# Mixer A's attention steps in an encoder block on eight Trainium2 cores: score of step k+1 issued before PV of step k

## The chip, the cores and the metric

The kernel runs on the eight cores of one Trainium2 chip, four on each of two dies. Every core runs the same program on its own 1024 tokens (a quarter of one of the two sequences) and needs nothing from the others while it runs. The metric is device time in microseconds (us) of the slowest core.

## The reference, cut to what matters

One layer of a bidirectional encoder: an adaLN-modulated RMSNorm, one wide input projection, two attention mixers, gates, an output projection, then a mixture of 64 experts. The change touches mixer A, dilated sliding-window attention with three head groups:

```python
A_PATTERNS = ((128, 1), (512, 4), (2048, 16))     # (window, dilation), 4 heads of 128 each

def dilated_attention(q, k, v, window, dilation):
    # tokens of one residue class modulo dilation form a sequence of their own
    o, lse = banded_attention(split(q), split(k), split(v), (window // 2) // dilation)
...
    # banded_attention: each query sees the keys at most 64 positions away
    sc = jnp.einsum('bhnqd,bhnkd->bhnqk', qb, kwin) * (hd ** -0.5)
    sc = jnp.where(valid, sc, NEG)
    lse = jax.nn.logsumexp(sc, axis=-1)
    p = jnp.exp(sc - lse[..., None])
    o = jnp.einsum('bhnqk,bhnkd->bhnqd', p, vwin)
...
w = jax.nn.softmax(jnp.stack(lses, axis=0), axis=0)           # the groups' weights
o = jnp.sum(w[..., None] * jnp.stack(outs, axis=0), axis=0)
```

The kernel keeps, for each group, the unnormalised sum of exp(score) x V and the sum of exp(score), adds both over the groups, and divides once at the end.

## The kernel before, in words

All data lies in one SBUF arena and eight PSUM banks. The program is written out in Python as five queues, one per engine; `P.op(engine, fn, reads, writes)` appends an instruction to the queue of its engine and works out from the buffers it reads and writes which counts of other engines it has to wait for. An engine runs its queue in the order in which the source appends to it; no scheduler moves anything. A wait stands in front of the instruction that needs it and holds up all that is behind it in that queue.

The stages, in order: conditioning vectors; normalised own tokens; mixer A; keys, values and attention of mixer B; gates and output projection; expert stage with the final norm.

Mixer A works in eight units: four of dilation 16 (four residue classes each), two of dilation 4 (two classes each), two of dilation 1. At the first unit of a dilation the queries are projected for all 1024 tokens. Then each unit projects keys and values, tile by tile of 128 keys (`run_pipeline`, matmuls on L447, transposes on L473), and only when they are all done comes the part that the change rewrites, L689 to L754: a loop over classes, heads h and key tiles m, one step for each. A step is

- S: a score matmul into bank `bi`, keys as rows, queries of one or two 64- or 128-wide blocks as columns (L704, TensorE);
- an exponential from PSUM into a bf16 buffer (L709, ScalarE);
- a multiplication by the band mask and the key-valid column (L718, VectorE);
- PV: for each block one matmul with V into bank 2 or 3 (L730) and one with a matrix of ones into bank 4 or 5 for the sum (L732), TensorE.

After the last key tile of a head the two PSUM results are evicted by ScalarE (L742, L744) into two scratch buffers, and VectorE copies (dilation 16: L747, L749) or adds them (L752, L754) to the accumulators `accO` and `accZ`. The steps per unit are 32 (16 class-heads of 2 key tiles), 24 (8 of 3) and 20 (4 of 5): 128 + 48 + 40 = 216 in all. Score banks 0 and 1, and the two exponential and two mask buffers, are chosen by `bi = (m + h) % 2`.

After the last unit VectorE forms the reciprocal of all of `accZ` (L762) and mixer B begins. Mixer B's own attention (score L871, exponential L874, PV L884 and L886) already issues the score matmul of a step before the PV of the step before it.

The weights of the projections come through a ring of three slots, loaded by GpSimd's queue (L118); a load waits for the matmuls that last read its slot.

Of the kernel before, what the change touches and what calls it, by code (L numbers as in the profile page):

```python
# [7 lines left out]
AF = mybir.ActivationFunctionType  # L8
ALU = mybir.AluOpType
# [11 lines left out]
SCALE = float(HD) ** -0.5  # L21
# [113 lines left out]
def build_nc(stop_after=None, dbg=None):  # L135
    nc = bass.Bass("TRN2", target_bir_lowering=False)
    P = Prog()
# [39 lines left out]
    def V(off, shape, dt=BF16):  # L177
        n = 1
        for s_ in shape[1:]:
            n *= s_  # L180
        assert off % 4 == 0
        assert off + n * (4 if dt == F32 else 2) <= ARENA * 2, (off, shape)
        if dt == F32:
            a = arena[:, off // 2: off // 2 + 2 * n].bitcast(F32)
        else:
            a = arena[:, off // 2: off // 2 + n]
        if len(shape) == 3:
            a = a.rearrange("p (a b) -> p a b", b=shape[2])
        elif len(shape) == 4:
            a = a.rearrange("p (a b c) -> p a b c", b=shape[2], c=shape[3])  # L190
        if shape[0] < 128:
            a = a[0:shape[0]]
        return a

    def emit(dump=None):
        if dump is not None:
            ap, tiles = dump
            ncol = ap.shape[1]
            P.dma("sp", "do", out_d[0:ap.shape[0], 0:ncol], ap, reads=tiles)
        for sn in list(P.cnt.keys()):  # L200
            P.final_wait("sp", sn)
        sem_names = ["pe", "act", "dve"] + ["sp_d%d" % i for i in range(24)] + ["pool_d%d" % i for i in range(24)]
        sems = {n_: es.enter_context(nc.semaphore("s_" + n_)) for n_ in sem_names}
        with nc.Block() as block:
            @block.tensor
            def _(e):
                P.replay("pe", e, sems)

            @block.scalar
            def _(e):  # L210
                P.replay("act", e, sems)

# [46 lines left out]
    t_const = T("const"); t_modT = T("modT"); t_A1 = T("A1"); t_A2 = T("A2"); t_cact = T("cact")  # L259
# [193 lines left out]
    tmp_t = [T("tmp%d" % i) for i in range(4)]  # L453
# [119 lines left out]
    PTA = VA + 8192  # L573
    EXA = PTA + 2048
# [16 lines left out]
    for (gi, items) in units:  # L591
# [6 lines left out]
        def ktsz(m, gi=gi):  # L598
            return 64 if (gi == 2 and m == 1) else 128
# [84 lines left out]
        if stop_after == 'kv':  # L684
            dd = V(ACCO, [128, 2048], F32); t_dd = T('dd')
            P.op('dve', lambda e: e.tensor_copy(out=dd[:, 0:1024], in_=kaT[:, 0, 0:1024]), reads=t_ka, writes=[t_dd])
            P.op('dve', lambda e: e.tensor_copy(out=dd[:, 1024:2048], in_=V(VA, [128, 1024])), reads=t_va, writes=[t_dd])
            return emit((dd, [t_dd]))
        for ii, (cl, b_lo, b_hi) in enumerate(items):  # L689
            qcol0 = cl * nq  # L690
            for h in range(4):
                ob = 2 + (h % 2)
                zb = 4 + (h % 2)
                for m in range(b_lo, b_hi + 1):
                    n = ktsz(m)
                    blocks = [bq for bq in (m - 1, m) if b_lo <= bq < b_hi]
                    c_lo = blocks[0] * qb
                    ncols = len(blocks) * qb
                    bi = (m + h) % 2
                    sb = pbank(bi)  # L700
                    kpos = ii * kstride + (m - b_lo) * 128

                    def f(e, n=n, c_lo=c_lo, ncols=ncols, sb=sb, h=h, qcol0=qcol0, kpos=kpos, kaT=kaT):
                        return e.matmul(sb[0:n, 0:ncols], lhsT=kaT[:, h, kpos:kpos + n],  # L704
                                        rhs=qaT[:, h, qcol0 + c_lo:qcol0 + c_lo + ncols], start=True, stop=True)
                    P.op("pe", f, reads=[t_ka[ii]] + t_qaT, writes=[PB[bi]])
                    ex = V(EXA + bi * 1024, [128, 512])[0:n, 0:ncols]
                    pt_ = V(PTA + bi * 1024, [128, 512])[0:n, 0:ncols]
                    P.op("act", lambda e, ex=ex, sb=sb, n=n, ncols=ncols: e.activation(  # L709
                        out=ex, in_=sb[0:n, 0:ncols], func=AF.Exp, scale=SCALE), reads=[PB[bi]], writes=[exa_t[bi]])  # L710
                    if len(blocks) == 2:
                        mk = mask2[0:n, 0:256]
                    elif blocks[0] == m:
                        mk = mask2[0:n, 128:128 + qb]
                    else:
                        mk = mask2[0:n, 0:qb]
                    kvc = cl * nkt + m
                    P.op("dve", lambda e, pt_=pt_, ex=ex, mk=mk, n=n, kvc=kvc, kvalid=kvalid: e.scalar_tensor_tensor(  # L718
                        out=pt_, in0=ex, scalar=kvalid[0:n, kvc:kvc + 1], in1=mk, op0=ALU.mult, op1=ALU.mult),
                        reads=[exa_t[bi], t_const], writes=[pta_t[bi]])  # L720
                    for bq in blocks:
                        col = bq * qb - c_lo
                        first = (m == bq)
                        last = (m == bq + 1)
                        po_ = pbank(ob)[:, (bq - b_lo) * qb:(bq - b_lo + 1) * qb]
                        pz_ = pbank(zb)[:, (bq - b_lo) * qb:(bq - b_lo + 1) * qb]
                        vv = vslot[(ii, m)]

                        def g(e, po_=po_, pz_=pz_, vv=vv, pt_=pt_, col=col, n=n, first=first, last=last, h=h, qb=qb):
                            e.matmul(po_, lhsT=vv[:, h * 128:(h + 1) * 128], rhs=pt_[:, col:col + qb],  # L730
                                     start=first, stop=last, skip_group_check=True)
                            return e.matmul(pz_, lhsT=ones_bf[0:n, :], rhs=pt_[:, col:col + qb], start=first,  # L732
                                            stop=last, skip_group_check=True)
                        P.op("pe", g, reads=[pta_t[bi], t_va[ii], t_const], writes=[PB[ob], PB[zb]])
                nqc = (b_hi - b_lo) * qb
                po_all = pbank(ob)[:, 0:nqc]
                pz_all = pbank(zb)[:, 0:nqc]
                dO = accO[:, h, :].rearrange("p (u c) -> p c u", c=r)[:, cl, b_lo * qb:b_hi * qb]
                dZ = accZ[:, h, :].rearrange("p (u c) -> p c u", c=r)[:, cl, b_lo * qb:b_hi * qb]
                eo = tmpv[0][:, 0:nqc]  # L740
                ez = tmpv[1][:, 0:nqc]
                P.op("act", lambda e, eo=eo, po_all=po_all: e.activation(out=eo, in_=po_all, func=AF.Identity),  # L742
                     reads=[PB[ob]], writes=[tmp_t[0]])
                P.op("act", lambda e, ez=ez, pz_all=pz_all: e.activation(out=ez, in_=pz_all, func=AF.Identity),  # L744
                     reads=[PB[zb]], writes=[tmp_t[1]])
                if gi == 2:
                    P.op("dve", lambda e, dO=dO, eo=eo: e.tensor_copy(out=dO, in_=eo),  # L747
                         reads=[tmp_t[0]], writes=[t_accO])
                    P.op("dve", lambda e, dZ=dZ, ez=ez: e.tensor_copy(out=dZ, in_=ez),  # L749
                         reads=[tmp_t[1]], writes=[t_accZ])  # L750
                else:
                    P.op("dve", lambda e, dO=dO, eo=eo: e.tensor_tensor(out=dO, in0=dO, in1=eo, op=ALU.add),  # L752
                         reads=[tmp_t[0]], writes=[t_accO])
                    P.op("dve", lambda e, dZ=dZ, ez=ez: e.tensor_tensor(out=dZ, in0=dZ, in1=ez, op=ALU.add),  # L754
                         reads=[tmp_t[1]], writes=[t_accZ])
        prev_kv_tiles = t_ka + t_va + pta_t + exa_t
        if stop_after == 'u0':
            return emit((accO[:, 0, :], [t_accO, t_accZ]))
# [529 lines left out]
```

How the kernel before makes its waits and increments, by code:

```python
    def replay(self, name, e, sems):  # L125
        for wl, fn, inc in self.q[name]:
            for k, v in wl:
                e.wait_ge(sems[k], v)
            if fn is None:
                continue
            ins = fn(e)
            ins.then_inc(sems[inc[0]], inc[1])
```

## Time and profile before

| | before |
|---|---|
| median of 6 runs | 9770.62 us (9679.11 to 10703.73) |
| the profiled execution, device time | 9680.7 us |
| its span, first to last instruction, slowest core | 9679.2 us |
| spans of the eight cores | 9651.3 to 9679.2 us |
| TensorE matmul busy | 7929.6 us, 82% |
| VectorE busy | 3593.4 us, 37% |
| ScalarE busy | 2132.8 us, 22% |
| mean granted TensorE clock, all cores | 0.934 to 0.935 |

How to read the rows further down: times are in us from the first instruction, unless ns is written. PE is TensorE's matmuls, PEld its weight loads, DVE VectorE, ACT ScalarE, POOL GpSimd. L730 is line 730 of the kernel before. A granted clock of 1.0 is 2.4 GHz, 0.5 is 1.2 GHz. In a timeline row the start time comes first, then the duration, engine, line, operation, output and input; in brackets how long the engine had been idle, and what ended that.

### The profile page before, as it was taken

The page shows a single profiled execution, that of the slowest core. Times are in us where ns is not written, and L with a number is a line of the kernel's source. Part 1 is how long each engine was busy: PE and PEld are TensorE (multiplying, and loading weights), DVE is VectorE, ACT ScalarE, POOL GpSimd, SP SyncE. Part 2 cuts the span into 40 slices and gives each one's busy share as a digit, 9 for nine tenths or more (in the row PEclk, how much of TensorE's full clock was granted, in tenths as well). Part 3 has the DMA queues.
Part 4 walks back from the last instruction along what each step waited for, and adds up shares of the span by engine and source line. Part 5 has one row for each costly group of instructions (what it writes and reads, how often), then busy time and mean ns, then how long its engine had stood idle before and what let it go on. Part 6 is the DMA issues. An engine that isn't in the chain of part 4 may idle for free.

```text
span 9679.2 us, 104693 instructions; the slowest of 8 cores (9651.3 to 9679.2 us)
## 1 busy us (share of the span) xinstructions
PE 7929.6 (82%) x37040; PEld 3549.6 (37%) x37040; DVE 3593.4 (37%) x4682; ACT 2132.8 (22%) x4075; POOL 289.0 (3%) x284
## 2 busy tenths in 40 slices
PE   0135656476777799759999999999999999999998
PEld 0122323232222234324444444444444444444443
DVE  3443334453111111244333334444444433334444
ACT  0124534465666651020000000000000000000001
POOL 0000000000000001000000000000000000000000
PEclk9997777688888999879999999999999999999999
DMA  7541123121000027534444444444444444444443
GB/s 207 170 136 36 48 63 77 56 68 45 13 4 13 9 21 74 90 54 73 76 79 74 73 73 78 79 79 79 79 79 76 74 78 76 73 73 75 79 79 83
DMA packets 505629, 694.53 MB, mean 72 GB/s; under 512 B 129440, under 2 KB 443296, under 8 KB 492960
## 3 DMA queue, kind: packets, MB, share of 16 engines
q0 software_dynamic: 451584, 476.37, 31.9%
q1 hardware_dynamic: 53536, 211.46, 6.7%
q8 instruction: 309, 5.06, 0.2%
q14 instruction: 200, 1.64, 0.1%
HBM read 1155.75 MB, written 8.39 MB: 120 GB/s over the span
## 4 chain that ended last, share of the span: by engine, by line
PE 72%; ACT 8%; DMA 7%; issue 6%; DVE 6%; ACTq 0%; DVEq 0%; SPq 0%; POOLq 0%; POOL 0%
PE psum L1151 37%; PE psum L1174 19%; PE psum L447 6%; PE psum L884 3%; DMA arena<-w_ada 3%; DMA arena<-w_in 2%; ACT arena L874 2%; PE psum L886 2%; PE psum L871 2%; DVE arena L398 2%; ACT arena L396 1%; PE psum L1026 1%; DVE arena L319 1%; DMA arena<-w_b_up 1%; ACT arena L376 1%
## 5 line engine op out<-in xcount | busy, mean ns | idle before, releaser
L1151 PE MATMUL psum<-arena 128*128 128x512 bf16 x16640 | 3603.2, 379 | 0.0
L1151 PEld LDWEIGHTS psum<-arena 128*128 128x128 bf16 x16640 | 1628.4, 98 | 1963.9 <-issue 1.6
L1174 PE MATMUL psum<-arena 128*128 128x512 bf16 x8320 | 1806.3, 379 | 0.0
L1179 DVE SCALAR_TENSOR_TENSOR arena<-psum,arena 128x512 f32<-128x512 f32 x2048 | 1533.0, 750 | 239.4 <-DVE arena L1179 14.5
L1161 DVE TENSOR_TENSOR arena<-arena,psum 128x512 bf16<-128x512 f32 x520 | 357.3, 687 | 2943.8 <-PE psum L1151 2943.8
L1159 ACT ACTIVATE arena<-psum 128x512 f32<-128x512 f32 x520 | 310.5, 597 | 5041.6 <-PE psum L1151 5041.6
L1174 PEld LDWEIGHTS psum<-arena 128*128 128x128 bf16 x8320 | 814.1, 98 | 981.7
L447 PE MATMUL psum<-arena 128*128 128x512 bf16 (+1 forms) x3648 | 923.6, 416 | 214.9 <-DVE arena L520 96.4
L874 ACT ACTIVATE arena<-psum 128x512 bf16<-128x512 f32 x1024 | 605.4, 597 | 296.0 <-PE psum L871 270.1
L447 PEld LDWEIGHTS psum<-arena 128*128 128x128 bf16 (+1 forms) x3648 | 383.4, 107 | 708.6 <-issue 374.7
L884 PE MATMUL psum<-arena 128*128 128x512 bf16 x1024 | 410.0, 400 | 266.8 <-ACT arena L874 251.4
L393 PE MATMUL psum<-arena 128*128 128x128 bf16 (+1 forms) x1504 | 118.4, 245 | 454.8 <-ACT arena L412 388.1
L886 PE MATMUL psum<-arena 128*128 128x512 bf16 x1024 | 408.7, 399 | 0.0
L871 PE MATMUL psum<-arena 128*128 128x512 bf16 x1024 | 407.1, 398 | 0.0
L884 PEld LDWEIGHTS psum<-arena 128*128 128x128 bf16 x1024 | 99.9, 98 | 684.8 <-issue 677.3
L118 POOL DMA_DIRECT2D arena<-w x192 | 195.0, 1016 | 5160.1 <-PE psum L1151 3494.8
L398 DVE TENSOR_TENSOR arena<-arena 128x2048 bf16<-128x2048 bf16 x94 | 198.3, 2110 | 346.8 <-ACT arena L396 346.8
L890 DVE RECIPROCAL arena<-psum 128x512 f32<-128x512 f32 x32 | 107.4, 3357 | 564.7 <-PE psum L886 564.7
L376 ACT ACTIVATE arena<-arena 128x2048 bf16<-128x2048 f32 x102 | 194.0, 1902 | 519.3 <-DMA arena<-xr 505.3
L319 DVE SCALAR_TENSOR_TENSOR arena<-arena 128x1536 f32<-128x1536 f32 x120 | 218.1, 1818 | 209.9 <-DMA arena<-w_ada 209.2
L730 PE MATMUL psum<-arena 128*128 128x128 bf16 (+2 forms) x256 | 58.7, 245 | 288.0 <-DVE arena L718 288.0
L329 PE MATMUL psum<-arena 128*128 128x1 f32 x192 | 41.2, 352 | 307.2 <-DVE arena L319 307.2
(119 smaller groups left out, 3822.4 us busy)
## 6 DMA issues: line engine op xcount, KB each, us to landing
arena<-w POOLq DMA_DIRECT2D x192, 2048.0 KB, 15.0
arena<-w_ada SPq DMA_DIRECT2D x128, 768.0 KB, 5.1
arena<-xr SPq DMA_DIRECT2D x78, 1024.0 KB, 5.0
arena<-w_in POOLq DMA_DIRECT2D x15, 2048.0 KB, 22.7
arena<-w_in POOLq DMA_DIRECT2D x32, 512.0 KB, 6.7
arena<-xr SPq DMA_DIRECT2D x16, 512.0 KB, 5.0
arena<-tabB SPq DMA_DIRECT2D x64, 128.0 KB, 2.0
arena<-w_b_up POOLq DMA_DIRECT2D x16, 512.0 KB, 6.7
```

The lines of the kernel that those rows point to most:

```text
L319: P.op("dve", lambda e, a=a, st=st, k=k: e.scalar_tensor_tensor(out=a, in0=st, scalar=c_act[:, k:k + 1], in1=a, op0=ALU.mult, op1=ALU.add) ...
L398: P.op("dve", lambda e: e.tensor_tensor(out=htmp[:, :, 0:n], in0=htmp[:, :, 0:n], in1=Asc.unsqueeze(2).to_broadcast([128, 16, n]), op=ALU. ...
L447: ins = e.matmul(po[0:n, :], lhsT=hT_ap[:, k, 0:n], rhs=wv[:, k, :], start=(k == 0), stop=(k == 15))
L871: P.op("pe", lambda e: e.matmul(pbank(sbk), lhsT=kbT[:, kvh, t * 128:(t + 1) * 128], rhs=qbT[:, hh, half * 512:(half + 1) * 512], start=Tr ...
L874: P.op("act", lambda e: e.activation(out=ptb[pi], in_=pbank(sbk), func=AF.Exp, scale=SCALE), reads=[PB[sbk]], writes=[ptb_t[pi]])
L884: e.matmul(pbank(ob), lhsT=vB[:, t, kvh * 128:(kvh + 1) * 128], rhs=ptb[pi], start=(t == 0), stop=(t == 31))
L886: return e.matmul(pbank(zb), lhsT=ones_bf, rhs=ptb[pi], start=(t == 0), stop=(t == 31))
L1151: ins = e.matmul(pbank(bank), lhsT=wsrc[:, k, fc * 128:(fc + 1) * 128], rhs=h2T[:, k, hs], start=(k == 0), stop=(k == 15))
L1159: P.op("act", lambda e, st=st, ba=ba: e.activation(out=st, in_=pbank(ba), func=AF.Silu), reads=[PB[ba]], writes=[stt])
L1161: P.op("dve", lambda e, st=st, bu=bu, fc=fc, hs=hs: e.tensor_tensor(out=hidT[:, fc, hs], in0=st, in1=pbank(bu), op=ALU.mult), reads=[stt, ...
L1174: ins = e.matmul(pbank(bank), lhsT=hidT[:, fc, j * 128:(j + 1) * 128], rhs=w2v[:, fc, cs], start=(fc == 0), stop=(fc == 3))
L1179: P.op("dve", lambda e, bank=bank, j=j, cs=cs, ex_i=ex_i: e.scalar_tensor_tensor(out=x1[:, j, cs], in0=pbank(bank), scalar=gate[:, j, ex_i ...
```

## The change

The nested loop becomes a flat list of steps and two functions. `S_step(k)` appends the score matmul, the exponential and the masking of step k; `PV_step(k)` appends its PV matmuls (now as one operation with one wait and one signal, where a step of two blocks had two) and, at the last key tile of a head, the evictions and accumulations. A last loop calls `S_step(k + 1)` ahead of `PV_step(k)`. The buffers alternate with the step's number. Shapes, operands and the number of instructions stay.

```diff
-        for ii, (cl, b_lo, b_hi) in enumerate(items):
-            qcol0 = cl * nq
-            for h in range(4):
-                for m in range(b_lo, b_hi + 1):
...
-                    bi = (m + h) % 2
...
-                    P.op("pe", f, reads=[t_ka[ii]] + t_qaT, writes=[PB[bi]])
...
-                    for bq in blocks:
...
-                        P.op("pe", g, reads=[pta_t[bi], t_va[ii], t_const], writes=[PB[ob], PB[zb]])
+        steps = []
+        for ii, (cl, b_lo, b_hi) in enumerate(items):
+            for h in range(4):
+                for m in range(b_lo, b_hi + 1):
+                    steps.append((ii, cl, b_lo, b_hi, h, m))
+
+        def S_step(k, steps=steps, kaT=kaT, t_ka=t_ka, kvalid=kvalid, qb=qb, nq=nq, nkt=nkt, kstride=kstride, ktsz=ktsz):
+            ii, cl, b_lo, b_hi, h, m = steps[k]
...
+            bi = k % 2
+            sb = pbank(bi)
...
+                 reads=[t_ka[ii]] + t_qaT, writes=[PB[bi]])
...
+            P.op("act", lambda e: e.activation(out=ex, in_=sb[0:n, 0:ncols], func=AF.Exp, scale=SCALE),
+                 reads=[PB[bi]], writes=[exa_t[bi]])
...
+                 reads=[exa_t[bi], t_const], writes=[pta_t[bi]])
+            return (pt_, blocks, c_lo, n, bi)
+
+        def PV_step(k, info, steps=steps, vslot=vslot, t_va=t_va, qb=qb, r=r, gi=gi):
+            ii, cl, b_lo, b_hi, h, m = steps[k]
+            pt_, blocks, c_lo, n, bi = info
+            ob = 2 + (h % 2)
+            zb = 4 + (h % 2)
...
+            P.op("pe", g, reads=[pta_t[bi], t_va[ii], t_const], writes=[PB[ob], PB[zb]])
+            if m == b_hi:
...
+                P.op("act", lambda e: e.activation(out=eo, in_=po_all, func=AF.Identity),
                     reads=[PB[ob]], writes=[tmp_t[0]])
...
+        infos = {0: S_step(0)}
+        for k in range(len(steps)):
+            if k + 1 < len(steps):
+                infos[k + 1] = S_step(k + 1)
+            PV_step(k, infos[k])
```

What moves, on TensorE, in the first dilation 4 unit (steps A, B, C of a head with score widths 128, 256, 128; L704 becomes L705, L730 and L732 become L739 and L741). Before, one head:

```order
L704 MATMUL psum<-arena 128x128
L730 MATMUL psum<-arena 128x128
L732 MATMUL psum<-arena 128x128
L704 MATMUL psum<-arena 128x256
L730 MATMUL psum<-arena 128x128
L732 MATMUL psum<-arena 128x128
L730 MATMUL psum<-arena 128x128
L732 MATMUL psum<-arena 128x128
L704 MATMUL psum<-arena 128x128
L730 MATMUL psum<-arena 128x128
L732 MATMUL psum<-arena 128x128
```

With the change, at the same place, from the score matmul of B to that of the next head's B:

```order
L705 MATMUL psum<-arena 128x256
L739 MATMUL psum<-arena 128x128
L741 MATMUL psum<-arena 128x128
L705 MATMUL psum<-arena 128x128
L739 MATMUL psum<-arena 128x128
L741 MATMUL psum<-arena 128x128
L739 MATMUL psum<-arena 128x128
L741 MATMUL psum<-arena 128x128
L705 MATMUL psum<-arena 128x128
L739 MATMUL psum<-arena 128x128
L741 MATMUL psum<-arena 128x128
L705 MATMUL psum<-arena 128x256
```

Before, the score matmul of a step stands directly in front of its own PV pair or pairs; now the PV of the step before stands between them.

On ScalarE, at the start of the first dilation 16 unit (exponential L709, now L710; evictions L742 and L744, now L753 and L755; a 64x64 exponential belongs to a head's second step). Before:

```order
L709 ACTIVATE arena<-psum 128x64
L709 ACTIVATE arena<-psum 64x64
L742 ACTIVATE arena<-psum 128x64
L744 ACTIVATE arena<-psum 128x64
L709 ACTIVATE arena<-psum 128x64
```

With the change:

```order
L710 ACTIVATE arena<-psum 128x64
L710 ACTIVATE arena<-psum 64x64
L710 ACTIVATE arena<-psum 128x64
L753 ACTIVATE arena<-psum 128x64
L755 ACTIVATE arena<-psum 128x64
L710 ACTIVATE arena<-psum 64x64
```

The first exponential of the next head has moved ahead of the two evictions of this one; the second still stands behind them. VectorE's queue (masking L718, now L719; copies L747 and L749, now L758 and L759) changes in the same way:

```order
L719 SCALAR_TENSOR_TENSOR arena<-arena 128x64
L719 SCALAR_TENSOR_TENSOR arena<-arena 64x64
L719 SCALAR_TENSOR_TENSOR arena<-arena 128x64
L758 COPY arena<-arena 128x64
L759 COPY arena<-arena 128x64
L719 SCALAR_TENSOR_TENSOR arena<-arena 64x64
```

The masking of the next head's first step stands ahead of the copies of this head, that of its second step behind them. The queues of GpSimd and SyncE, which issue the DMAs, do not change.

## Rows read from the trace of the kernel before

**Rows 1.** Windows by stage: span, length, busy per engine (x instructions), PEclk, DMA share, GB/s.
```profile
620.00:1850.00 1230.00, 726.34 (x4099) 372.75 (x4098) 457.73 (x971) 560.89 (x1053) 9.38 (x8) 0.73 0.23 57
```

**Rows 2.** Windows of three score stretches, columns PE, PEld, DVE, ACT, POOL, PEclk, DMA, GB/s.
```profile
772.00:825.00 53.00, 14.44 (x100) 8.19 (x100) 15.27 (x64) 15.59 (x71) 0.00 (x0) 0.53 0.00 1
1394.00:1449.00 55.00, 14.13 (x90) 7.36 (x87) 17.71 (x40) 15.30 (x46) 0.00 (x0) 0.52 0.00 1
1797.00:1844.00 47.00, 13.31 (x83) 7.28 (x83) 13.21 (x28) 12.72 (x30) 0.00 (x0) 0.50 0.18 30
```

**Rows 3.** Waits from 700 to 1900 us: in total, times, longest.
```profile
PE psum L730 <- DVE arena L718: 288.0, 216, 3.7
```

**Rows 4.** Timeline of a dilation 16 unit: start, duration, engine, instruction, idle before.
```profile
788.54 0.21 PE L730 MATMUL psum<-arena 128*128 128x64 bf16 x1 [1.28 <-DVE arena L718]
...
789.84 0.21 PE L730 MATMUL psum<-arena 64*128 64x64 bf16 x1 [0.84 <-DVE arena L718]
...
790.03 0.23 PE L704 MATMUL psum<-arena 128*128 128x64 bf16 x1
...
790.64 0.22 ACT L709 ACTIVATE arena<-psum 128x64 bf16<-128x64 f32 x1
...
791.11 0.28 DVE L718 SCALAR_TENSOR_TENSOR arena<-arena 128x64 bf16<-128x64 bf16 x1
...
791.54 0.21 PE L730 MATMUL psum<-arena 128*128 128x64 bf16 x1 [1.28 <-DVE arena L718]
```

**Rows 5.** Timeline of a dilation 4 unit, first PV matmul of steps C, A, B, C.
```profile
1541.42 0.26 PE L730 MATMUL psum<-arena 128*128 128x128 bf16 x1 [1.22 <-DVE arena L718]
...
1543.90 0.27 PE L730 MATMUL psum<-arena 128*128 128x128 bf16 x1 [2.00 <-DVE arena L718]
...
1545.94 0.27 PE L730 MATMUL psum<-arena 128*128 128x128 bf16 x1 [1.46 <-DVE arena L718]
...
1547.86 0.26 PE L730 MATMUL psum<-arena 128*128 128x128 bf16 x1 [1.22 <-DVE arena L718]
```

**Rows 6.** Timeline of a dilation 1 unit, first PV matmul of steps A to E, A.
```profile
1810.67 0.26 PE L730 MATMUL psum<-arena 128*128 128x128 bf16 x1 [2.39 <-DVE arena L718]
...
1812.73 0.27 PE L730 MATMUL psum<-arena 128*128 128x128 bf16 x1 [1.46 <-DVE arena L718]
...
1814.99 0.26 PE L730 MATMUL psum<-arena 128*128 128x128 bf16 x1 [1.46 <-DVE arena L718]
...
1817.25 0.27 PE L730 MATMUL psum<-arena 128*128 128x128 bf16 x1 [1.46 <-DVE arena L718]
...
1819.16 0.27 PE L730 MATMUL psum<-arena 128*128 128x128 bf16 x1 [1.22 <-DVE arena L718]
...
1822.03 0.27 PE L730 MATMUL psum<-arena 128*128 128x128 bf16 x1 [2.39 <-DVE arena L718]
```

**Rows 7.** Timeline of GpSimd's queue, one row; then windows of the stretch behind it.
```profile
1227.18 1.14 POOL L118 DMA_DIRECT2D arena<-w_in  x1 [2.31 <-PE psum L473]
...
1240.00:1250.00 10.00, 2.64 (x18) 1.50 (x18) 3.44 (x15) 2.90 (x15) 0.00 (x0) 0.50 1.22 197
1250.00:1260.00 10.00, 3.06 (x21) 1.77 (x21) 2.96 (x13) 2.34 (x12) 0.00 (x0) 0.50 0.13 22
```

**Rows 8.** Timeline of VectorE after the last score stretch.
```profile
1844.42 25.75 DVE L762 RECIPROCAL arena<-arena 128x4096 f32<-128x4096 f32 x1
```

**Rows 9.** Groups by line and shape: busy, mean ns of one, idle before.
```profile
L874 ACT ACTIVATE arena<-psum 128x512 bf16<-128x512 f32 x1024 | 605.4, 597 | 296.0 <-PE psum L871 270.1 <-ACT arena L874 1.1 <-PE psum L886 0.7
...
L742 ACT ACTIVATE arena<-psum 128x512 f32<-128x512 f32 x8 | 4.8, 597 | 9.6 <-PE psum L732 9.6
```

**Rows 10.** Window in mixer B's attention, columns as in the other windows.
```profile
2400.00:2500.00 100.00, 72.36 (x277) 24.31 (x276) 17.14 (x22) 62.32 (x127) 0.00 (x0) 0.87 0.02 5
```

**Rows 11.** Timeline of TensorE, score matmuls at the full and the half clock.
```profile
1527.11 0.22 PE L704 MATMUL psum<-arena 128*128 128x128 bf16 x1
...
1541.59 0.31 PE L704 MATMUL psum<-arena 128*128 128x128 bf16 x1
```

More of the change, by code:

```diff
@@ L688, in build_nc @@
             return emit((dd, [t_dd]))
+        steps = []
         for ii, (cl, b_lo, b_hi) in enumerate(items):
-            qcol0 = cl * nq
-            for h in range(4):
-                ob = 2 + (h % 2)
-                zb = 4 + (h % 2)
-                for m in range(b_lo, b_hi + 1):
[L695 to L698, printed above, removed]
-                    bi = (m + h) % 2
[L700 to L705, printed above, removed]
-                    P.op("pe", f, reads=[t_ka[ii]] + t_qaT, writes=[PB[bi]])
[L707 to L720, printed above, removed]
-                    for bq in blocks:
[L722 to L733, printed above, removed]
-                        P.op("pe", g, reads=[pta_t[bi], t_va[ii], t_const], writes=[PB[ob], PB[zb]])
@@ new lines, in build_nc @@
+            for h in range(4):
[3 more added lines that the diff above has]
+            ii, cl, b_lo, b_hi, h, m = steps[k]
+            n = ktsz(m)
+            blocks = [bq for bq in (m - 1, m) if b_lo <= bq < b_hi]
+            c_lo = blocks[0] * qb
+            ncols = len(blocks) * qb
+            bi = k % 2
+            sb = pbank(bi)
+            kpos = ii * kstride + (m - b_lo) * 128
+            qcol0 = cl * nq
+            P.op("pe", lambda e: e.matmul(sb[0:n, 0:ncols], lhsT=kaT[:, h, kpos:kpos + n],
+                                          rhs=qaT[:, h, qcol0 + c_lo:qcol0 + c_lo + ncols], start=True, stop=True),
+                 reads=[t_ka[ii]] + t_qaT, writes=[PB[bi]])
+            ex = V(EXA + bi * 1024, [128, 512])[0:n, 0:ncols]
+            pt_ = V(PTA + bi * 1024, [128, 512])[0:n, 0:ncols]
+            P.op("act", lambda e: e.activation(out=ex, in_=sb[0:n, 0:ncols], func=AF.Exp, scale=SCALE),
+                 reads=[PB[bi]], writes=[exa_t[bi]])
+            if len(blocks) == 2:
+                mk = mask2[0:n, 0:256]
+            elif blocks[0] == m:
+                mk = mask2[0:n, 128:128 + qb]
+            else:
+                mk = mask2[0:n, 0:qb]
+            kvc = cl * nkt + m
+            P.op("dve", lambda e: e.scalar_tensor_tensor(out=pt_, in0=ex, scalar=kvalid[0:n, kvc:kvc + 1], in1=mk,
+                                                         op0=ALU.mult, op1=ALU.mult),
+                 reads=[exa_t[bi], t_const], writes=[pta_t[bi]])
+            return (pt_, blocks, c_lo, n, bi)
@@ new lines, in PV_step, with g @@
+        def PV_step(k, info, steps=steps, vslot=vslot, t_va=t_va, qb=qb, r=r, gi=gi):
[3 more added lines that the diff above has]
+            zb = 4 + (h % 2)
+            vv = vslot[(ii, m)]
+            def g(e):
+                ins = None
+                for bq in blocks:
+                    col = bq * qb - c_lo
+                    first = (m == bq)
+                    last = (m == bq + 1)
+                    po_ = pbank(ob)[:, (bq - b_lo) * qb:(bq - b_lo + 1) * qb]
+                    pz_ = pbank(zb)[:, (bq - b_lo) * qb:(bq - b_lo + 1) * qb]
+                    e.matmul(po_, lhsT=vv[:, h * 128:(h + 1) * 128], rhs=pt_[:, col:col + qb],
+                             start=first, stop=last, skip_group_check=True)
+                    ins = e.matmul(pz_, lhsT=ones_bf[0:n, :], rhs=pt_[:, col:col + qb], start=first,
+                                   stop=last, skip_group_check=True)
+                return ins
+            P.op("pe", g, reads=[pta_t[bi], t_va[ii], t_const], writes=[PB[ob], PB[zb]])
+            if m == b_hi:
@@ L741, in build_nc @@
                 ez = tmpv[1][:, 0:nqc]
-                P.op("act", lambda e, eo=eo, po_all=po_all: e.activation(out=eo, in_=po_all, func=AF.Identity),
+                P.op("act", lambda e: e.activation(out=eo, in_=po_all, func=AF.Identity),
                      reads=[PB[ob]], writes=[tmp_t[0]])
-                P.op("act", lambda e, ez=ez, pz_all=pz_all: e.activation(out=ez, in_=pz_all, func=AF.Identity),
+                P.op("act", lambda e: e.activation(out=ez, in_=pz_all, func=AF.Identity),
                      reads=[PB[zb]], writes=[tmp_t[1]])
                 if gi == 2:
-                    P.op("dve", lambda e, dO=dO, eo=eo: e.tensor_copy(out=dO, in_=eo),
+                    P.op("dve", lambda e: e.tensor_copy(out=dO, in_=eo), reads=[tmp_t[0]], writes=[t_accO])
+                    P.op("dve", lambda e: e.tensor_copy(out=dZ, in_=ez), reads=[tmp_t[1]], writes=[t_accZ])
+                else:
+                    P.op("dve", lambda e: e.tensor_tensor(out=dO, in0=dO, in1=eo, op=ALU.add),
                          reads=[tmp_t[0]], writes=[t_accO])
-                    P.op("dve", lambda e, dZ=dZ, ez=ez: e.tensor_copy(out=dZ, in_=ez),
+                    P.op("dve", lambda e: e.tensor_tensor(out=dZ, in0=dZ, in1=ez, op=ALU.add),
                          reads=[tmp_t[1]], writes=[t_accZ])
[L751 to L755, printed above, removed]
+        infos = {0: S_step(0)}
[3 more added lines that the diff above has]
+            PV_step(k, infos[k])
         prev_kv_tiles = t_ka + t_va + pta_t + exa_t
```

## The prediction, made before the changed kernel was run

> **What bounds the kernel now.** I read the table by stage first, because the change touches one stage only. The front of the layer, 620 to 1850 us, is 1230 us long and TensorE is busy for 726 us of it at a mean granted clock of 0.73 [rows 1]: no engine bounds it, so it must be bound by waits between engines. Then I looked for the eight stretches in it that hold the mixer A score and PV steps, one per unit. Three of them stand in [rows 2], each marked out from the first score matmul to the last accumulate: 53 us for one of the four units of dilation 16 (the others are 51 to 52), 55 us for one of the two of dilation 4 (the other too), 47 us for one of the two of dilation 1 (the other 48). Together that is some 412 us. In each, TensorE, VectorE and ScalarE are each busy for 13 to 18 us out of about 50, and the granted clock is 0.50 to 0.53, the lower of the two levels (1.2 GHz). A third of the time for each of three engines is the picture of a chain in which one works while the others wait. The table of waits names the last link: TensorE waited 216 times, 288 us in all, for the masking on VectorE before a PV matmul [rows 3]. 216 is the number of steps (128 + 48 + 40).
>
> The timeline shows the chain instruction by instruction. In a dilation 16 unit a head has two steps. From the PV of the first to the PV of the second is 1.30 us (788.54 to 789.84); from there to the next head's first PV it is 1.70 us (789.84 to 791.54), because the ScalarE queue holds the two evictions before the next exponential (790.64) and the VectorE queue the two copies before the next masking (791.11) [rows 4]. So a head costs 3.00 us. In a dilation 4 unit the three steps A, B, C of a head give C to next A 2.48, A to B 2.04, B to C 1.92, together 6.44 us [rows 5]. In a dilation 1 unit the five steps A to E give 2.06, 2.26, 2.26, 1.91 and, over the evictions, 2.87, together 11.36 us [rows 6]. Each of these intervals is one full pass: PV, score matmul, exponential, masking, PV.
>
> **The change, part by part.** It adds and removes no arithmetic. Each score matmul, exponential and masking is put one step earlier in the three queues, ahead of the PV of the step before. The interval that I called one pass now leads from PV(k) to PV(k+2): behind PV(k) on TensorE stands S(k+2), then the exponential and the masking of k+2, and PV(k+2) waits for that. Two such chains, of the even and the odd steps, run interleaved. Nothing else becomes a dependence: the score banks and the two pairs of intermediate buffers already alternate, and S(k+2) writes the bank whose reader, the exponential of k, was done before PV(k) could start.
>
> Dilation 16, 64 heads in four units. With two steps a head, the odd chain carries every eviction, so its pass stays 1.70 us; the even chain needs 1.30 us and fits beside it. A head costs 1.70 instead of 3.00 us. Per unit, before: 1.30 + 15 x 3.00 = 46.3 us from first to last PV. After: an estimated 0.4 us from PV 0 to PV 1 (a PV and a score matmul, 0.19 each in [rows 4]; the chains start together, with no eviction there yet), then 15 x 1.70, together 25.9. Saved 20.4 per unit, 81.6 in four.
>
> Dilation 4, 16 heads in two units. With three steps a head, a chain takes every second step: A to C, C to the next head's B, B to the A after that. In two heads that is three passes, one over an eviction, one from each kind of step; I take the three intervals of [rows 5] for them, 6.44 us, though a pass over the eviction now lands on the wider B and one from A on the narrower C, which moves tenths from one link to another. So a head costs 3.22. Before: 2.04 + 1.92 + 7 x 6.44 = 49.0 us; after about 1.7 + 7 x 3.22 = 24.2. Saved 24.8 per unit, 49.6 in two.
>
> Dilation 1, 8 heads in two units. In the same way a chain needs two heads for its five passes, and a head costs 11.36 / 2 = 5.68. Before: 8.5 + 3 x 11.36 = 42.6; after A to C to E, 4.0, + 3 x 5.68 = 21.0. Saved 21.6 per unit, 43.1 in two.
>
> **Sum:** 81.6 + 49.6 + 43.1 = 174 us, so that the 412 us become 238. The table load and first step of each unit and its last eviction stay as they are. One PV operation per step instead of one per query block takes a semaphore increment off TensorE in 40 steps; I cost that at nothing, since the masking before it ends the wait.
>
> What lies behind the score stretches comes earlier by the same amounts, and I looked for what it could run into. Two 2 MB weight loads are issued just before the last dilation 16 stretch begins, the later at 1227, and have landed soon after 1250: the DMA share is 1.22 from 1240 to 1250 and 0.13 after that [rows 7]. Before, that stretch ends at 1280; after the change, 20 us sooner, near 1260, and the loads feed the key and value projections, which come after the query projections. The same pair exists before the last dilation 4 stretch. After the last stretch VectorE has its 25.75 us reciprocal [rows 8] with TensorE idle; it moves forward whole and covers what the last weight load still needs. The long expert stage is untouched. So all of it arrives at the end.
>
> The unknown cost is what a link takes when the other chain works beside it; no row of these stretches shows it. From below it is the link as measured. From above I take the links that already have other work in the queue: 1.70 against 1.30, 2.48 against 1.92, 2.87 against 1.91. The nearest row for an instruction is in mixer B, which does issue one step ahead: its exponential of 128x512 takes 597 ns, as does the 128x512 eviction of mixer A with nothing beside it [rows 9]. I therefore take the links as measured.
>
> The clock is the other unknown. The stretch of [rows 2] has TensorE 14.44 of 53 us busy, 27%, at 0.53; mixer B has 72% busy at 0.87 [rows 10]. After the change it would be 14.4 of about 32, 46%. That is nearer to the 27% row, so I leave the clock where it is. The page "TensorE: Matmul & The Clock Gate" of the Trainium skill, Part 1: The HAM clock gate, says that the slow rate is the default and sustained activity releases it. By that rule the denser stretch could run at 2.4 GHz and the sum would be the first rival's; by the rows it is 174 us.
>
> **The rivals.**
> 1. The clock rises in the denser stretches. The score matmul 128x128 takes 0.22 us at the full clock and 0.31 at half [rows 11], and the step from PV to the score matmul would halve too (0.19 in [rows 4], more with two blocks): about 0.25 us a link. One chain has 108 links, so 27 us more are gained: 9479 us. For it: the share goes from 27 to 46%. Against: it is still far from 72%.
> 2. Each head's evictions hold up both chains, not one. The exponential of k+1 is ahead of the evictions in the queue, but if it comes late, the chains fall into step and lose their interleaving. Priced: 0.65 us per dilation 16 head (a second pass of 1.30, half hidden), 64 x 0.65 = 42; 0.56 per dilation 4 head and 0.96 per dilation 1 head, 9 + 8; together 59, which leaves 115 us of gain: 9565 us. Against it: VectorE, the busiest of the two, has 15.27 us of work in what would be 32.
> 3. The program order changes but the waits stay as serial as now, since they count instructions of an engine and not buffers. Then the time is as before, 9681. Against it: the listing shows S(k+1) and its exponential ahead of everything that depends on PV(k).
> 4. Slower. All three engines now touch the score buffers and PSUM in the same microsecond; if that lengthens their instructions and handovers, the score stretches, 238 us by the links, pass 412 + 20 us only from a factor of 1.8 on. At a factor of 1.9 the time would be 9721. Against it: the two 597 ns of [rows 9].
>
> **How the numbers follow.** The profiled execution took 9680.7 us (span 9679.2); 9680.7 - 174 = 9506 us, against that execution and not against the median of the runs shown, which is 90 us above it; the three lowest of the six runs lie within 4 us. My chances: forecast 0.67, rival 1 0.15, rival 2 0.12, rival 3 0.03, rival 4 0.03. Low end: rival 1 with a little more, 9470. High end: half of the gain lost, 87 us, beyond rival 2 and short of rival 3: 9595. Faster by over 0.2% (19 us, about what a measurement of this kernel can tell from no change) are the first three, 0.94; within it 0.03; slower 0.03.
>
> **What would show it.** The eight score stretches should be about 31, 30 and 26 us long by dilation; TensorE's wait for the masking should fall from 288 to near 115 us. In the timeline of a dilation 16 unit PV to PV should alternate between some 0.4 and 1.3 us, with 1.70 a head; an exponential should start before the PV of the step before it. The stretches between should keep their lengths. The prediction is wrong if a head of dilation 16 takes over 2.3 us, if the clock leaves 0.5, or if the stage behind a score stretch starts with a wait for a load that it did not have.

## The result, and the profile after

| | before | with the change |
|---|---|---|
| median of all runs | 9861.73 us (20 runs) | 9538.78 us (10 runs) |
| lowest run | 9675.03 us | 9501.16 us |
| profiled execution, device time | 9680.7 us | 9506.79 us |
| ratio to the kernel before | | 0.9843, 95% interval 0.98 to 0.9886 |
| eight score stretches, slowest core | 412 us | 239.6 us |

In many runs the cores of one die, or of both, show a lower granted clock and a longer span, with any of the kernels, so the medians hold such runs; below, spans and score stretches are those of a die without them. A score stretch is, as in [rows 2], the time from the first score matmul of a unit to its last accumulate.

The profiled execution fell by 174 us, which was the forecast. On each core the eight score stretches became 172 us shorter; on the slowest core the first of them also began 3 us earlier than before, at 769.6 in place of 772.6 us, and what runs before it is not touched by the change. The windows of one stretch of each dilation, which answer to [rows 2] (columns PE, PEld, DVE, ACT, POOL, PEclk, DMA share, GB/s):

```profile
769.00:801.00 32.00, 12.13 (x100) 7.47 (x100) 14.55 (x64) 14.92 (x71) 0.00 (x0) 0.54 0.01 2
1311.00:1342.00 31.00, 12.77 (x90) 7.81 (x86) 16.69 (x40) 14.83 (x46) 0.00 (x0) 0.56 0.00 1
1643.00:1671.00 28.00, 12.46 (x84) 7.94 (x84) 13.75 (x29) 14.06 (x33) 0.00 (x0) 0.50 0.30 51
```

From first score matmul to last accumulate the eight take 31.3, 31.6, 31.1 and 31.0, then 30.9 and 30.9, then 26.4 and 26.4 us. The instructions per engine are the same as in [rows 2] (in the first, 100, 64 and 71 on TensorE, VectorE and ScalarE); the length is not. The clock is still the lower one. TensorE's wait for the masking, 288 us in [rows 3], is now (in total, times, longest):

```profile
PE psum L739 <- DVE arena L719: 124.4, 121, 3.6
```

It was forecast near 115 us. It has fallen from 216 times to 121: most PVs of the other chain no longer wait. The timeline of a dilation 16 unit shows it (start, duration, engine, instruction; idle time before it in brackets), one head and the start of the next, to be held against [rows 4]:

```profile
785.72 0.21 PE L739 MATMUL psum<-arena 64*128 64x64 bf16 x1 [0.97 <-DVE arena L719]
...
785.91 0.26 PE L705 MATMUL psum<-arena 128*64 128x64 bf16 x1
...
786.11 0.23 PE L739 MATMUL psum<-arena 128*128 128x64 bf16 x1
...
786.19 0.22 ACT L753 ACTIVATE arena<-psum 128x64 f32<-128x64 f32 x1 [0.94 <-PE psum L705]
...
786.53 0.42 ACT L710 ACTIVATE arena<-psum 64x64 bf16<-64x64 f32 x2
...
787.00 0.53 DVE L719 SCALAR_TENSOR_TENSOR arena<-arena 64x64 bf16<-64x64 bf16 x2
...
787.42 0.21 PE L739 MATMUL psum<-arena 64*128 64x64 bf16 x1 [0.97 <-DVE arena L719]
```

From the PV that ends a head (785.72) to the next one that does (787.42) are 1.70 us, the length of the pass over the evictions in [rows 4]; the first-step PV follows 0.39 us behind (786.11) without a wait. Two exponentials and two maskings now run as pairs ("x2") behind the evictions. The same for dilation 4 and dilation 1 (the first PV matmul of a head's second step, one head apart; the row at 1322.92 is the first head's step C, used further down):

```profile
1322.44 0.26 PE L739 MATMUL psum<-arena 128*128 128x128 bf16 x1 [0.94 <-DVE arena L719]
...
1322.92 0.31 PE L739 MATMUL psum<-arena 128*128 128x128 bf16 x1
...
1325.77 0.26 PE L739 MATMUL psum<-arena 128*128 128x128 bf16 x1 [0.94 <-DVE arena L719]
...
1653.29 0.27 PE L739 MATMUL psum<-arena 128*128 128x128 bf16 x1 [1.41 <-DVE arena L719]
...
1659.15 0.27 PE L739 MATMUL psum<-arena 128*128 128x128 bf16 x1 [1.11 <-DVE arena L719]
```

A head costs 3.33 us (forecast 3.22, before 6.44 by [rows 5]) and 5.86 (forecast 5.68, before 11.36 by [rows 6]).

Nothing is given back. From the first score to the last accumulate the slowest core took 1071.7 us before and 900.5 with the change. On average over the eight cores what lies between the eight stretches takes 660 us before and after, what lies between the last accumulate and the expert stage 2407 and 2408 us, and the expert stage 5361 us in both. A window of it with the change, all matmuls:

```profile
4026.00:9326.00 5300.00, 5252.03 (x24397) 2384.85 (x24397) 2167.55 (x2663) 325.74 (x531) 191.90 (x189) 0.99 0.46 76
```

### The profile page after: what moved, and what is told of

Read it like the earlier page. It is cut to its first block, busy times and chain, and to the rows that moved or that the text cites. A ratio compares the mean times of both kernels' runs of the same rounds, so it can differ in the third digit from the quotient of the medians.

```text
span 9505.2 us, 105002 instructions; the slowest of 8 cores (9470.2 to 9505.2 us)
## 1 busy us (share of the span) xinstructions
PE 7908.0 (83%) x37040; PEld 3547.2 (37%) x37040; DVE 3589.4 (38%) x4682; ACT 2127.4 (22%) x4075; POOL 289.0 (3%) x284
## 4 chain that ended last, share of the span: by engine, by line
PE 73%; ACT 8%; DMA 8%; issue 5%; DVE 5%; ACTq 0%; DVEq 0%; SPq 0%; POOLq 0%; POOL 0%
PE psum L1165 38%; PE psum L1188 19%; PE psum L447 6%; DMA arena<-w_ada 3%; PE psum L898 3%; ACT arena L888 2%; DMA arena<-w_in 2%; PE psum L900 2%; DVE arena L398 2%; PE psum L885 2%; ACT arena L396 1%; PE psum L1040 1%; DVE arena L319 1%; DMA arena<-w_b_up 1%; ACT arena L376 1%
## 5 line engine op out<-in xcount | busy, mean ns | idle before, releaser
L1153 DVE TENSOR_TENSOR arena<-arena 128x8192 bf16<-128x8192 bf16 x65 | 287.0, 4415 | 0.0
```

## The experiments

The theory: a score stretch is a chain of passes, and the gain is that a pass now leads two steps on. Its rivals: the gain came with the other edits; an engine binds; the clock rose. All runs, with the mean length of a score stretch by dilation and the sum of the eight, and the median span of a die's cores (the mean of the two dies where both can be used). The spans carry some noise of their own, since the first score stretch starts anywhere from 750 to 784 us; the sums of the stretches agree within 0.5 us from core to core.

| run | dilation 16, 4, 1 (us) | sum | span |
|---|---|---|---|
| before | 51.7, 55.1, 47.6 | 412 | 9664 |
| with the change | 31.3, 30.9, 26.4 | 239.6 | 9493 |
| e1 order undone, rest kept | 55.6, 55.3, 47.6 | 428.3 | 9677 |
| e2 evictions a step later | 28.6, 31.5, 25.6 | 228.7 | 9483 |
| e3 two steps ahead | 22.3, 26.7, 20.6 | 183.7 | 9429 |
| e5 extra matmuls | 31.4, 30.9, 26.4 | 240.0 | 9494 |
| e9 as e1, late wait last | 49.0, 51.1, 43.7 | 385.5 | 9621 |
| e7 the change, late wait last | 28.2, 29.4, 25.0 | 221.7 | 9467 |
| e8 as e3, late wait last | 19.7, 25.0, 19.5 | 167.7 | 9414 |
| e10 as e8, whole program | 19.7, 24.9, 19.8 | 168.1 | 9385 |
| e12 before, late wait last, whole program | 48.8, 51.4, 43.7 | 385.4 | 9594 |
| e11 is e10 again | the same | 167.9 | 9387 |

**The order alone undone.**

```diff
-        infos = {0: S_step(0)}
         for k in range(len(steps)):
-            if k + 1 < len(steps):
-                infos[k + 1] = S_step(k + 1)
-            PV_step(k, infos[k])
+            PV_step(k, S_step(k))
```

> The changed kernel with the order alone undone: each step's score part is issued directly before its own PV part; the buffers by step number and the single PV operation per step stay. Chain theory (the gain is that a pass PV to score to exponential to masking leads to the step after next): the eight score stretches go back to about 52, 55 and 48 us by dilation, 412 in all, and the time to 9680 us, ratio 1.00 against the kernel before. Rival (part of the gain is in what rode along, fewer waits per step and alternating buffers): the stretches stay well under 412, say 330 to 390, and the time 25 to 90 us under the kernel before.

The stretches went back beyond 412, to 428.3 us: the gain is the order's, and what rode along costs 16 us, all of it in dilation 16, 0.25 us a head. The second step of a head shows where. Before (score matmul, exponential, masking; the PVs at both ends, 788.54 and 789.84, stand in [rows 4]):

```profile
788.74 0.26 PE L704 MATMUL psum<-arena 128*64 128x64 bf16 x1
789.10 0.22 ACT L709 ACTIVATE arena<-psum 64x64 bf16<-64x64 f32 x1 [1.23 <-PE psum L704]
789.41 0.28 DVE L718 SCALAR_TENSOR_TENSOR arena<-arena 64x64 bf16<-64x64 bf16 x1 [1.02 <-ACT arena L709]
```

In this run (PV of the first step, score matmul, exponential, masking, PV):

```profile
787.00 0.21 PE L739 MATMUL psum<-arena 128*128 128x64 bf16 x1 [1.27 <-DVE arena L719]
...
787.20 0.26 PE L705 MATMUL psum<-arena 128*64 128x64 bf16 x1
787.67 0.22 ACT L710 ACTIVATE arena<-psum 64x64 bf16<-64x64 f32 x1 [1.34 <-PE psum L705]
788.13 0.28 DVE L719 SCALAR_TENSOR_TENSOR arena<-arena 64x64 bf16<-64x64 bf16 x1 [1.27 <-ACT arena L710]
788.55 0.21 PE L739 MATMUL psum<-arena 64*128 64x64 bf16 x1 [1.09 <-DVE arena L719]
```

The pass takes 1.55 us (787.00 to 788.55) where [rows 4] have 1.30: score matmul to exponential 0.47 in place of 0.36, exponential to masking 0.46 in place of 0.31. The listing of the queues with their waits, for the exponential and the masking of that step, before and in this run:

```
L709 ACTIVATE arena<-psum 64x64 [waits s_pe]
L718 SCALAR_TENSOR_TENSOR arena<-arena 64x64 [waits s_act]

L710 ACTIVATE arena<-psum 64x64 [waits s_pe,s_act,s_dve]
L719 SCALAR_TENSOR_TENSOR arena<-arena 64x64 [waits s_act,s_dve,s_pe]
```

With `bi = (m + h) % 2` the buffers of the dilation 16 steps ran 0, 1, 1, 0, 0, 1, 1, 0: the second step of a head took the buffer that the first step of the head before had used, and a count waited for earlier covered it. With `k % 2` it takes the buffer of the step two before, which no earlier wait covers: two more waits on each of the two instructions, met long ago, but standing behind the one that comes late. That gave a new theory, tried further down.

**Evictions a step later.** The part of `PV_step` from `if m == b_hi` on becomes `EV_step`:

```diff
             PV_step(k, infos[k])
+            if k >= 1:
+                EV_step(k - 1)
+        for k in range(len(steps) - 1, len(steps)):
+            EV_step(k)
```

> The changed kernel with each head's two evictions and two accumulations issued one step later, behind the exponential and masking of the step after next. Chain theory (evictions lie in the pass of the odd chain): a head costs about 1.35 to 1.45 us in dilation 16 in place of 1.70, 3.0 in place of 3.33 in dilation 4, 5.4 in place of 5.86 in dilation 1; the stretches add up to some 210 us in place of 240 and the time is about 9477. Rival (ScalarE or VectorE throughput already sets the step): no change, 240 and 9507.

Between the two: 11 us gained where 30 were expected, and dilation 4 got 0.6 us a unit longer. In dilation 16 most heads of the first unit now take 1.54 or 1.55 us. One pass of the first steps' chain:

```profile
779.94 0.21 PE L739 MATMUL psum<-arena 128*128 128x64 bf16 x1 [0.62 <-ACT arena L758]
...
780.07 0.21 PE L705 MATMUL psum<-arena 128*128 128x64 bf16 x1
...
780.49 0.22 ACT L710 ACTIVATE arena<-psum 128x64 bf16<-128x64 f32 x1 [0.45 <-DVE arena L763]
...
780.95 0.29 DVE L719 SCALAR_TENSOR_TENSOR arena<-arena 128x64 bf16<-128x64 bf16 x1 [0.40 <-PE psum L705]
...
781.49 0.21 PE L739 MATMUL psum<-arena 128*128 128x64 bf16 x1 [0.63 <-ACT arena L758]
```

So the evictions did lie in the pass of the change, 1.70 us, and without them it is about what a pass without evictions took in the first run, 1.55. The expectation had started from the 1.30 of [rows 4], which lacks the added waits: 0.42 us from score matmul to exponential and 0.46 to the masking are 0.21 more than there. Another 0.11 lie between masking and PV (0.54 in place of 0.43), where the PV's wait ends, by the trace, with the eviction L758 that frees its bank; PV to score matmul is 0.07 less. This kernel was not run with another order of waits. In dilation 4 the move only shifted the load: a head takes 3.35 us in place of 3.33, and the second of its two additions is now directly followed on VectorE, with no idle time, by the masking of a later step.

```profile
1322.72 0.59 DVE L768 TENSOR_TENSOR arena<-arena 128x256 f32<-128x256 f32 x1
1323.23 0.33 DVE L719 SCALAR_TENSOR_TENSOR arena<-arena 128x128 bf16<-128x128 bf16 x1
```

**Two steps ahead.** Three score banks (0, 1, 6), three pairs of intermediate buffers:

```diff
-            bi = k % 2
-            sb = pbank(bi)
+            bi = k % 3
+            sbi = (0, 1, 6, 7)[bi]
+            sb = pbank(sbi)
...
-        infos = {0: S_step(0)}
+        infos = {j: S_step(j) for j in range(2)}
         for k in range(len(steps)):
-            if k + 1 < len(steps):
-                infos[k + 1] = S_step(k + 1)
+            if k + 2 < len(steps):
+                infos[k + 2] = S_step(k + 2)
```

> The changed kernel with the score part issued two steps ahead, three score banks and three pairs of intermediate buffers. Chain theory: the same pass now leads to the third step, so a dilation 16 head costs (1.30 + 1.70) / 3 = 1.00 us in place of 1.70, or 1.1 if VectorE's 0.92 us of work per head begins to bind; dilation 4: 2.2 to 2.4 in place of 3.33 (VectorE has 2.09 us of work per head); dilation 1: 3.8 to 4.1 in place of 5.86. Stretches about 170 us, time about 9437. Rival (an engine or the in-order queues bind after one step of lookahead): under 15 us gained, over 9490.

183.7 us, 56 gained where the pure chain gave 70: after the change the passes still bound, no engine did. In a dilation 16 stretch of 22 us VectorE and ScalarE are now busy for 13 each, but that they filled up is not what kept the 14 us back: with the same work a further run below gains 16 by the order of the waits alone.

**Extra matmuls, for the clock.** Ahead of the second PV of each dilation 16 head:

```diff
+            if gi == 2 and steps[k][5] == steps[k][2]:
+                def warm(e):
+                    for _ in range(2):
+                        ins = e.matmul(pbank(7)[:, 0:512], lhsT=ones_bf, rhs=hT_own[:, 0, 0:512], start=True, stop=True)
+                    return ins
+                P.op("pe", warm, reads=[t_const] + hto_t, writes=[PB[7]])
             PV_step(k, infos[k])
```

> The changed kernel with two extra matmuls of 128x512 into an idle bank ahead of the second PV of each head in dilation 16 only, where TensorE waits 0.97 us a head anyway; they do work that nothing reads. If activity sets the clock, the granted clock of the four dilation 16 stretches rises from 0.54 to over 0.8, and at a price of 0.2 us a pass their length falls from 31.3 to about 28 us each. If the clock stays at 0.54, the extra matmuls take 0.85 us of the 0.97 and the stretches stay at 31 to 33 us. The four stretches of dilation 4 and 1 stay as they are in both cases, 30.9 and 26.4.

The window of the first stretch:

```profile
769.00:800.00 31.00, 24.75 (x127) 10.92 (x126) 14.87 (x64) 14.61 (x70) 0.00 (x0) 0.53 0.01 2
```

TensorE is busy for 24.75 of 31 us in place of 12.13 of 32, and the granted clock is 0.53; the stretch keeps its length, 31.4 us against 31.3. At its start TensorE waits 2.85 us (to 772.41); from there to the last PV it is never idle for more than 0.47 us at a time, and from 771 to 800 us the granted clock is 0.50. What a link would cost at the full clock was therefore not measured.

**Order of waits, serial kernel.** A single edit in how the waits of one instruction are listed, switched on for mixer A's steps:

```diff
-        for t in reads:
-            if t.w is not None:
-                need(*t.w)
+        if not self.reads_last:
+            for t in reads:
+                if t.w is not None:
+                    need(*t.w)
         for t in writes:
...
+        if self.reads_last:
+            for t in reads:
+                if t.w is not None:
+                    need(*t.w)
```

> The serial kernel of the first run (428 us of score stretches: 16 us more than before, all in dilation 16) with one more edit, in mixer A's steps alone: where an instruction waits for several counts, the wait for the operand that it reads, which comes last, is put behind the waits for the buffer that it overwrites, which were met long before. The same waits stay. Wait-order theory (each wait that stands behind the late one costs about 0.07 us, and the change added two of them to the exponential and two to the masking of every second step in dilation 16): exponential to masking falls from 0.46 to about 0.32 us, score matmul to exponential from 0.47 to 0.36, in every step; some 0.25 us per step, 216 steps, so the stretches take about 375 us, dilation 16 about 48 each. Rival (the order of waits is free, and the 16 us come from the banks and buffers themselves): 428 us, no change.

385.5 us in place of 428.3: 43 gained of the 53 expected. The same instructions as above:

```profile
778.28 0.21 PE L746 MATMUL psum<-arena 128*128 128x64 bf16 x1 [1.10 <-DVE arena L726]
...
778.47 0.26 PE L712 MATMUL psum<-arena 128*64 128x64 bf16 x1
778.83 0.22 ACT L717 ACTIVATE arena<-psum 64x64 bf16<-64x64 f32 x1 [1.16 <-PE psum L712]
779.15 0.28 DVE L726 SCALAR_TENSOR_TENSOR arena<-arena 64x64 bf16<-64x64 bf16 x1 [1.02 <-ACT arena L717]
779.57 0.21 PE L746 MATMUL psum<-arena 64*128 64x64 bf16 x1 [0.84 <-DVE arena L726]
```

Score matmul to exponential 0.36 (was 0.47), exponential to masking 0.32 (was 0.46): the pass takes 1.29 us (778.28 to 779.57), as in [rows 4], with the same three waits on each as in the first run. Two waits behind the late one cost 0.11 and 0.14 us here.

**Order of waits, the change.** The same edit.

> The changed kernel with the same edit of the order of waits in mixer A's steps. Wait-order theory: each of the 108 passes on a chain gets some 0.25 us shorter, less where the instruction sits in the queue behind an eviction: a dilation 16 head about 1.40 us in place of 1.70, dilation 4 about 3.0 in place of 3.33, dilation 1 about 5.3 in place of 5.86; stretches about 212 us in place of 240, time about 9479. Rival (order is free): 240 and 9507.

221.7 us: 18 gained of the 28 expected. One dilation 16 head, PV to PV of the second steps, is 1.52 us in place of 1.70. That instructions behind an eviction gain less, as the expectation allowed, fits this, but no run shows it by itself:

```profile
768.26 0.21 PE L746 MATMUL psum<-arena 64*128 64x64 bf16 x1 [0.80 <-DVE arena L726]
...
769.78 0.21 PE L746 MATMUL psum<-arena 64*128 64x64 bf16 x1 [0.80 <-DVE arena L726]
```

**Order of waits, two steps ahead.** The same edit on the kernel of e3.

> The kernel with the score part two steps ahead (184 us of score stretches) with the same edit of the order of waits in mixer A's steps. If the passes still bind with three chains, a third of 0.25 us per step is gained, 216 x 0.08 = 18 us: about 166 us. If an engine's queue binds instead (VectorE has 0.92 us of work per head in dilation 16 and the head takes about 1.36), under 5 us are gained, 180 or more, unless the waits themselves fill the queue, and then the gain is larger, down to about 155.

167.7 us, 16 gained of the 18 expected. A dilation 16 head is down to 0.95 us (PV of first steps):

```profile
776.16 0.21 PE L747 MATMUL psum<-arena 128*128 128x64 bf16 x1
...
777.11 0.21 PE L747 MATMUL psum<-arena 128*128 128x64 bf16 x1
```

**Order of waits in the whole program.** On the kernel of e3, and on the kernel before; the reads simply follow the writes for every instruction.

> The kernel with the score part two steps ahead and the order of waits turned round in the whole program, not in mixer A's steps alone. The score stretches should equal those of the kernel with the edit in mixer A alone. Outside, about 2300 us of the program are bound by handovers (key and value production, mixer B's attention, where TensorE waits 251 us for the exponential in 1024 steps): at 0.07 us per wait behind the late one, 20 to 100 us are gained. If the order is free, nothing: the time is that of two steps ahead, about 9450.

> The kernel before, in its serial order, with the order of waits alone turned round in the whole program. Wait-order theory: the score stretches go from 412 to about 385 us, what the serial kernel with the late wait last had (there the two added waits no longer cost anything, so both kernels meet), and outside them some 25 us are gained, as between the two kernels with two steps ahead: about 9630 us on an undisturbed die against 9680. If the order matters only where steps overlap: 412 and 9680.

The score stretches came out as expected, 168.1 and 385.4 us. The second equals the 385.5 of the serial kernel with the late wait last: in that order of waits the two serial kernels meet, so the 16 us between them (428.3 and 412) were the place of the added waits and nothing else that rode along. Outside the stretches, measured from the first score matmul to the end as a mean over cores, the edit gave 29 us between e8 and e10 (8651 to 8622) and some 40 on the kernel before (8900 to 8833, less 27 in the stretches). Of these, 31 and 37 us lie between the last accumulate of mixer A and the expert stage; the expert stage gained nothing.

**The best version, once more.**

> The kernel with the score part two steps ahead and the late wait last in the whole program, once more, for a ratio against the kernel before. From its first look: 168 us of score stretches, about 9400 us on undisturbed dies, ratio 0.971 against the kernel before; the changed kernel stands at 0.982.

The medians of the two dies' spans were 9385.9 and 9388.0 us. The lowest of six runs took 9400.52 us; the three lowest runs of the kernel before beside it took 9668.49, 9669.19 and 9670.83: 0.972. That rests on one run of the best version, and no interval was given for it.

## What the prediction had right, and the step that failed

- **The bound.** Right: undoing the order alone brings the stretches back (e1), and a further step of lookahead shortens them again (e3), with the same instructions. A chain of passes, not an engine, set the time.
- **The 174 us.** Right: 172 measured in the stretches. By dilation, 16 first, the forecast was 81.6, 49.6 and 43.1 us; measured were 81.6, 48.4 and 42.4. That the profiled execution took 9506.79 us, within 1 us of the 9506 forecast, is luck in part: 3 us of its 174 are the earlier start of the first stretch.
- **The step that failed: the base of the sum.** The prediction took 174 us off 9680.7 us, the time of one execution, "against that execution and not against the median of the runs shown", and gave the forecast in microseconds alone. The term that was mis-sized is that base: the 20 runs of the kernel before have a median of 9861.73 us, 181 more, and even the median of the six runs that the prediction had was 90 more. Against 9861.73 the 9506 stand for 3.6% less, twice what the 174 us are worth; the runs showed a ratio of 0.9843, 1.6% less (interval 1.1 to 2.0%). What the sum supported was the ratio of its own two numbers, 0.982, which lies in the measured interval: the five lowest runs with the change took 9501 to 9511 us, the eight lowest before 9675 to 9683. The median of the ten runs with the change, 9538.78 us, is 33 us above the forecast and inside the range.
- **"Nothing else becomes a dependence."** True of the data, false of the waits. Nor did the banks and buffers "already alternate" in dilation 16, where the last step of a head and the first of the next used the same one. The new buffer rule added two waits to the exponential and two to the masking of every second step in dilation 16. Serial, that costs 16 us (e1). The prediction did not cost it at all. What it costs in the changed kernel was not measured by itself; there these instructions stand behind the evictions, and the pass that holds them takes the forecast 1.70 us.
- **Dilation 16.** The step is right: 1.70 us a head, with the odd chain carrying every eviction; PV to PV alternates between 0.39 and 1.31 as forecast.
- **Dilations 4 and 1.** The mechanism is right, the size off by 0.11 and 0.18 us a head. The two chains did not run freely beside each other: in dilation 4 the pass from C over the eviction to the next B takes 2.85 us (1322.92 to 1325.77), and the C of that head then follows its B by 0.49, since TensorE takes PVs in order: 3.33 together. Over both dilations that is 2.6 us; the unit ends gave back less than 1, and the rest is the 2 us between 174 and 172.
- **Rival 1, the clock.** It did not rise: 0.54, 0.56 and 0.50 in the three windows, 0.53, 0.52 and 0.50 in [rows 2]. The reason given for that, the distance to mixer B's 72%, was weak, though: in e5 TensorE was busy for 80% of the stretch, and the clock stayed too. So the rule of the Trainium skill, page "TensorE: Matmul & The Clock Gate", Part 1: The HAM clock gate, that activity releases the higher rate, was not borne out by these two stretches, busy for 38% and 80%; why the clock stays there is open.
- **Rival 2, evictions hold both chains.** It had 0.65 us more for a dilation 16 head, 2.35 us; the head takes 1.70. In e2, with the evictions moved, it takes 1.55.
- **Rival 3, no overlap,** is excluded by the pairs in the timeline, **rival 4, longer instructions,** by the durations: the masking of 128x256 took 479 ns on average with the change and 484 before, the exponential of the same width 393 and 384.

## What to carry to other kernels

Where three engines are each a third busy, time one full pass from a handover to the same handover: issued one step ahead, that pass spans two steps. Here the gain followed from the passes, with what sits in the queues on the way counted in (172 of 174 us); for the second step of lookahead the passes alone promised too much (56 of 70). State such a gain as a ratio, or against a base that is measured in the same way as the result. Then look at what each instruction waits for: a buffer rule can add waits without adding a dependence, and where several counts are waited for, the one that comes last belongs at the end of the list. A second step of lookahead was worth another 56 us and the order of waits 16, so the first gain was not the last.

## What the runs showed that was not expected

Waits that are long met are not free when they stand behind the late one: the exponential started 0.11 us and the masking 0.14 us earlier with the same three waits in another order (e1 against e9), and over the whole program that is another 29 or 40 us outside the score stretches (e8 to e10, before to e12). And a TensorE that is busy for 24.75 of 31 us kept a granted clock of 0.53 (e5).
